# Sums over later key tiles in the third layer: from totals made by VectorE instead of one matmul for each tile

## The reference

```python
def stick_breaking_attention(q, k, v):
    """q, k, v: (B, H, S, Dh). Strictly causal stick-breaking attention, 128-query blocks.
    A[t,s] = sigmoid(z_ts) * prod_{s<j<t} (1 - sigmoid(z_tj)), s < t, evaluated in log space."""
    S = q.shape[2]
    outs = []
    for i in range(S // BLOCK_Q):
        q0, q1 = i * BLOCK_Q, (i + 1) * BLOCK_Q
        qb = q[:, :, q0:q1]
        kb = k[:, :, :q1]
        vb = v[:, :, :q1]
        z = jnp.einsum('bhqd,bhkd->bhqk', qb, kb).astype(jnp.float32) * SB_SCALE
        q_pos = jnp.arange(q0, q1)[:, None]
        k_pos = jnp.arange(q1)[None, :]
        mask = k_pos < q_pos
        log_1m_beta = jnp.where(mask, -jax.nn.softplus(z), 0.0)
        suffix = lax.cumsum(log_1m_beta, axis=3, reverse=True) - log_1m_beta
        w = jnp.where(mask, jnp.exp(jax.nn.log_sigmoid(z) + suffix), 0.0)
        outs.append(jnp.einsum('bhqk,bhkd->bhqd', w.astype(vb.dtype), vb))
    return jnp.concatenate(outs, axis=2)
```

## Time and profile before

| | |
|---|---|
| median of 3 runs | 1201.03 us (1200.93, 1201.03, 2348.67) |
| profiled execution, its own time | 1200.89 us |
| its span, first to last instruction | 1199.1 us |
| PE busy, share of the span | 1188.1 us, 99% |
| DVE busy | 631.9 us, 53% |
| ACT busy | 559.5 us, 47% |
| POOL busy | 415.9 us, 35% |
| granted TensorE clock, mean | 1.000 |

### The profile page before, as it was taken

How to read it: one execution, slowest core, us unless ns; L and a number is a source line. 1 busy time by engine, 2 the same in 40 slices (tenths; PEclk the granted TensorE clock), 3 DMA queues, 4 the chain that set the end, 5 groups by cost and what they waited for, 6 DMA issues and landing times.

```text
span 1199.1 us, 19184 instructions
## 1 busy us (share of the span) xinstructions
PE 1188.1 (99%) x7763; PEld 1019.4 (85%) x7763; DVE 631.9 (53%) x1099; ACT 559.5 (47%) x1071; POOL 415.9 (35%) x295
## 2 busy tenths in 40 slices
PE   8999999999999999999999999999999999999998
PEld 7799879998987778889999888888888888888898
DVE  4587644787577477887370435454442851004434
ACT  5535245535532387886454445454544123344234
POOL 2434331110053255652304323333223553443441
PEclk9999999999999999999999999999999999999999
DMA  8325514557465311002223222212221323323321
GB/s 260 111 71 177 173 36 133 185 170 198 98 130 115 62 36 36 2 2 54 71 71 106 71 71 71 70 40 68 72 71 36 116 95 106 105 88 105 105 71 72
DMA packets 131265, 111.76 MB, mean 93 GB/s; under 512 B 38834, under 2 KB 128048, under 8 KB 131184
## 3 DMA queue, kind: packets, MB, share of 16 engines
q1 hardware_dynamic: 129696, 106.92, 30.7%
q10 hardware_dynamic: 1488, 3.71, 1.4%
HBM read 104.85 MB, written 2.10 MB: 89 GB/s over the span
## 4 chain that ended last, share of the span: by engine, by line
PE 94%; DVE 3%; ACT 2%; DMA 1%; issue 0%; POOL 0%; SPq 0%; ACTq 0%; DVEq 0%
PE banks L1421 43%; PE banks L1410 13%; PE banks L1444 6%; PE banks L1868 4%; PE banks L1886 3%; PE banks L1511 3%; PE banks L2020 3%; PE banks L1849 3%; PE banks L1909 2%; PE banks L2059 2%; PE banks L1982 1%; PE banks L2090 1%; PE banks L1386 1%; PE banks L1581 1%; PE banks L1733 1%; PE banks L1635 1%
## 5 line engine op out<-in xcount | busy, mean ns | idle before, releaser
L672 POOL TENSOR_TENSOR w_lo<-raw,w_hi 128x1024 fp32r<-128x1024 f32 x130 | 325.2, 2522 | 612.3 <-ACT w_hi L775 612.2
L1421 PE MATMUL banks<-act_hi,w_hi 128*128 128x512 f32 x704 | 277.7, 394 | 0.1
L1421 PE MATMUL banks<-act_lo,w_hi 128*128 128x512 f32 x704 | 274.6, 390 | 0.0
L1421 PE MATMUL banks<-act_hi,w_lo 128*128 128x512 f32 x704 | 274.6, 390 | 0.0
L775 ACT ACTIVATE w_hi<-raw 128x1024 fp32r<-128x1024 f32 (+1 forms) x156 | 154.9, 1043 | 124.9 <-PE banks L1421 97.5
L1421 PEld LDWEIGHTS banks<-act_hi,w_hi 128*128 128x128 f32 x704 | 132.4, 188 | 28.2 <-issue 1.4
L1421 PEld LDWEIGHTS banks<-act_lo,w_hi 128*128 128x128 f32 x704 | 132.2, 188 | 28.0
L1421 PEld LDWEIGHTS banks<-act_hi,w_lo 128*128 128x128 f32 x704 | 132.4, 188 | 26.3
L1410 PE MATMUL banks<-w_hi,act_hi 128*128 128x256 f32 x384 | 109.3, 285 | 0.1
L1410 PE MATMUL banks<-w_hi,act_lo 128*128 128x256 f32 x384 | 108.8, 283 | 0.0
L1410 PE MATMUL banks<-w_lo,act_hi 128*128 128x256 f32 x384 | 108.8, 283 | 0.0
(11 more groups left out here) (449 smaller groups left out, 2459.9 us busy)
## 6 DMA issues: line engine op xcount, KB each, us to landing
raw<-w_in SPq DMA_DIRECT2D x32, 1024.0 KB, 5.7
raw<-gla_w_in SPq DMA_DIRECT2D x11, 1024.0 KB, 5.3
raw<-nsa_w_in SPq DMA_DIRECT2D x29, 256.0 KB, 4.5
raw<-nsa_w_in SPq DMA_DIRECT2D x6, 1024.0 KB, 6.6
raw<-gla_w_out SPq DMA_DIRECT2D x4, 1024.0 KB, 6.6
ada_first<-w_ada SPq DMA_DIRECT2D x4, 1024.0 KB, 8.1
raw<-nsa_w_out SPq DMA_DIRECT2D x16, 256.0 KB, 5.1
raw<-w_branch_a SPq DMA_DIRECT2D x4, 1024.0 KB, 5.0
```

Of the source, the lines that this page charges most:

```text
L672: pool.tensor_tensor(w_lo[:, u, k], raw[:, u, k], w_hi[:, u, k].bitcast(F32), ALU.subtract).then_inc(lo_done, 1)
L1421: mm = pe.matmul(b[:], w[:, u, k, m * P:(m + 1) * P], x[:, k, :], start=(k == 0 and n == 0), stop=(k == KT - 1 and n == 2))
```

## The change

`later2` is new: for each head, key tile 2 for query tile 2, and key tile 2 plus key tile 3 for query tile 3. `later1` is key tile 1 plus `later2`, over query tiles 1 to 3. VectorE makes both by two copies and two additions as soon as groups 1 and 2 have their maxima, ahead of their high and low parts and, in pairs 0, 2 and 4, ahead of `query_low`. ScalarE rounds both to `later2_hi` and `later1_hi` between `pair_split(p - 1)` and `take3(c, 1)`, and VectorE makes `later2_lo` and `later1_lo` after group 0's low part. For each head and each of high and low, `head_sums` then needs one matmul with `minus_r` for key tile 1, where two stood (key tiles 2 and 3), and one for key tile 0, where three stood (key tiles 1, 2 and 3). These two sets of four come last in `head_sums`, and each has a wait of its own on `sp_ready`. The new tiles lie in memory of `mix_a` (pairs 0 to 5) and of `qh`, `kh`, `vh` (pairs 6 and 7) that is idle then.

```diff
--- before.py
+++ after.py
@@ -270,6 +270,18 @@
         pool_fix = sb("pool_fix", [P, 4, 16])
         sp_lo = over("sp_lo", [P, 5, S], ln_z, F32R)
         w_z = over("w_z", [P, 5, S], sp_hi)
+
+        def later_parts(name, width, at, last_at, dt=F32R):
+
+            return [over(f"{name}{i}", [P, 2, width], mix_a, dt, at=b)
+                    for i, b in enumerate((mix_a.manual_sbuf_range[0] + 4 * at, last_at))]
+
+        later1_hi = later_parts("later1_hi", 3 * P, 0, qh.manual_sbuf_range[0])
+        later1_lo = later_parts("later1_lo", 3 * P, 6 * P, kh.manual_sbuf_range[0])
+        later1 = later_parts("later1", 3 * P, 6 * P, kh.manual_sbuf_range[0], F32)
+        later2_hi = later_parts("later2_hi", 2 * P, 12 * P, vh.manual_sbuf_range[0])
+        later2_lo = later_parts("later2_lo", 2 * P, 16 * P, vh.manual_sbuf_range[0] + 4 * 4 * P)
+        later2 = later_parts("later2", 2 * P, 16 * P, vh.manual_sbuf_range[0] + 4 * 4 * P, F32)
         pool_u = over("pool_u", [P, KT, S], qh)
         silu_zb = over("silu_zb", [P, KT, S], vh)
         mix_b = over("mix_b", [P, KT, S], ln_z)
@@ -1290,7 +1302,7 @@
                 split_high(c + 1, (c + 1) // 2, (c + 1) % 2)
                 for i, g in enumerate((1, 2, 0)):
 
-                    act.wait_ge(zc_ready, 3 * p + i + 1)
+                    act.wait_ge(zc_ready, 4 * p + i + 1)
                     act.activation(group(ln_z, g), group(ln_z, g), ACT.Exp).then_inc(e_ready, 1)
                 for i, g in enumerate((1, 2, 0)):
                     act.wait_ge(e_ready, 3 * p + i + 1)
@@ -1298,6 +1310,9 @@
                 take3(c, 0)
                 if p:
                     pair_split(p - 1)
+                act.wait_ge(zc_ready, 4 * p + 4)
+                for high, total in ((later2_hi, later2), (later1_hi, later1)):
+                    act.activation(high[p >= 6][:], total[p >= 6][:], ACT.Copy).then_inc(l_ready, 1)
                 take3(c, 1)
                 split_high(c + 2, (c + 2) // 2, (c + 2) % 2)
                 if p % 2 == 0 or p == 7:
@@ -2020,31 +2035,37 @@
                 return pe.matmul(blocks(z_banks, a, st, skip=jt - st), (tri_r if jt == st else minus_r)[:],
                                  blocks((sp_hi, sp_lo)[n], a, jt), start=False, stop=stop, skip_group_check=True)
 
+            def later_sum(a, st, part, p, stop):
+
+                return pe.matmul(blocks(z_banks, a, st, skip=1), minus_r[:], part[p >= 6][:, a], start=False, stop=stop,
+                                 skip_group_check=True)
+
             def head_sums(p):
 
-                pe.wait_ge(sp_ready, 3 * (p + 1))
-                for jt in (3, 2):
-                    for n, part in enumerate((sp_hi, sp_lo)):
-                        pe.matmul(both_heads(z_banks, 2, skip=jt - 2), (tri_r if jt == 2 else minus_r)[:],
-                                  both_heads(part, jt), start=False, stop=(jt == 2 and n == 1), skip_group_check=True)
-                        if jt == 2:
-                            for a in range(2):
-                                source_sum(a, 0, 3, n)
-                for a in range(2):
-                    for n in range(2):
-                        source_sum(a, 1, 2, n)
-                        mm = source_sum(a, 0, 2, n)
+                pe.wait_ge(sp_ready, 5 * p + 3)
+                for part in (sp_hi, sp_lo):
+                    pe.matmul(both_heads(z_banks, 2, skip=1), minus_r[:], both_heads(part, 3),
+                              start=False, stop=False, skip_group_check=True)
+                for n, part in enumerate((sp_hi, sp_lo)):
+                    mm = pe.matmul(both_heads(z_banks, 2), tri_r[:], both_heads(part, 2), start=False, stop=(n == 1),
+                                   skip_group_check=True)
                 mm.then_inc(tri_full, 1)
                 for a in range(2):
                     for n in range(2):
                         source_sum(a, 1, 1, n)
                         source_sum(a, 3, 3, n, stop=(n == 1))
-                        source_sum(a, 0, 1, n)
-                        mm = source_sum(a, 1, 3, n, stop=(n == 1))
-                mm.then_inc(tri_full, 1)
                 for a in range(2):
                     for n in range(2):
-                        mm = source_sum(a, 0, 0, n, stop=(n == 1))
+                        source_sum(a, 0, 0, n)
+                pe.wait_ge(sp_ready, 5 * p + 4)
+                for a in range(2):
+                    for part in (later2_hi, later2_lo):
+                        mm = later_sum(a, 1, part, p, stop=(part is later2_lo))
+                mm.then_inc(tri_full, 1)
+                pe.wait_ge(sp_ready, 5 * p + 5)
+                for a in range(2):
+                    for part in (later1_hi, later1_lo):
+                        mm = later_sum(a, 0, part, p, stop=(part is later1_lo))
                 mm.then_inc(tri_full, 1)
 
             def head_values(p):
@@ -2652,6 +2673,12 @@
                 dve.wait_ge(qk_high, 4 * j + m + 3)
                 dve.tensor_tensor(br_lo[:, 2 * j + m], b, kh[:, j % 2, m].bitcast(F32), ALU.subtract)                    .then_inc(bank_free[2 * ((C_H + 1) % 2) + m], 1)
 
+            def source_split(g):
+
+                link(dve.tensor_copy(group(sp_hi, g), group(ln_z, g)))
+                dve.tensor_tensor(group(sp_lo, g), group(ln_z, g), group(sp_hi, g).bitcast(F32),
+                                  ALU.subtract).then_inc(sp_ready, 1)
+
             for m in range(2):
                 query_low(0, m, bank[2 * (C_H % 2) + m])
             for m in range(2):
@@ -2661,15 +2688,27 @@
 
                     dve.wait_ge(z_full, 3 * p + i + 1)
                     dve.tensor_scalar(group(ln_z, g), group(z_banks, g), CAP, None, ALU.min).then_inc(zc_ready, 1)
-                for i, g in enumerate((1, 2, 0)):
-
-                    if i == 2 and p % 2 == 0 and p < 6:
-                        query_low(p // 2 + 1, 0, bank[0])
-                    dve.wait_ge(l_ready, 3 * p + i + 1)
+                later = (p >= 6)
+                for i, g in enumerate((1, 2)):
+                    dve.wait_ge(l_ready, 5 * p + i + 1)
                     link(dve.tensor_tensor(group(ln_z, g), group(ln_z, g), group(z_banks, g), ALU.max))
-                    link(dve.tensor_copy(group(sp_hi, g), group(ln_z, g)))
-                    dve.tensor_tensor(group(sp_lo, g), group(ln_z, g), group(sp_hi, g).bitcast(F32),
-                                      ALU.subtract).then_inc(sp_ready, 1)
+                source3, source2 = both_heads(ln_z, 3), ln_z[:, 4].rearrange("p (a c) -> p a c", a=2)
+                from2, from1 = later2[later][:], later1[later][:]
+                dve.tensor_copy(from2[:, :, 0:P], source2[:, :, 0:P])
+                link(dve.tensor_tensor(from2[:, :, P:2 * P], source2[:, :, P:2 * P], source3, ALU.add))
+                dve.tensor_copy(from1[:, :, 0:P], ln_z[:, 2:4, 0:P])
+                link(dve.tensor_tensor(from1[:, :, P:3 * P], ln_z[:, 2:4, P:3 * P], from2, ALU.add))
+                dve.sem_inc(zc_ready, 1)
+                for g in (1, 2):
+                    source_split(g)
+                if p % 2 == 0 and p < 6:
+                    query_low(p // 2 + 1, 0, bank[0])
+                dve.wait_ge(l_ready, 5 * p + 3)
+                link(dve.tensor_tensor(group(ln_z, 0), group(ln_z, 0), group(z_banks, 0), ALU.max))
+                source_split(0)
+                for n, (high, low, total) in enumerate(((later2_hi, later2_lo, from2), (later1_hi, later1_lo, from1))):
+                    dve.wait_ge(l_ready, 5 * p + 4 + n)
+                    dve.tensor_tensor(low[later][:], total, high[later][:].bitcast(F32), ALU.subtract).then_inc(sp_ready, 1)
                 if p % 2 == 0 and p < 6:
                     query_low(p // 2 + 1, 1, bank[1])
                 if p:
```

## The result

The changed kernel takes 1208.28 us (median of 5 runs, 1206.61 to 1209.51) against 1200.93 (median of 5, one of which, 2348.67, again stands apart): ratio 1.0061, with a 95% interval of 1.0047 to 1.0075. It is slower, by about 0.6%; the interval leaves out 1, so this is measured, though the prediction counted anything under 2% as no change. The time is inside the forecast range of 1194 to 1211 and 1.6 us above the forecast of 1206.7.

The account below looks back on a forecast made before the run. TensorE was taken as the only limit in the changed stretch; 9.9 us saved against 15.65 lost to waits made it 5.75 us slower, forecast 1206.7 us, range 1194 to 1211.

Parts of the forecast that it names:

- The saving: TensorE's sums: fewer matmuls save 1.24 us for a pair, 9.9 for eight; upper bound 1.45 a pair.
- ScalarE's copies: Two copies ahead of taking product(c)'s second half, about 0.6 and 0.8 us, hidden with 1.1 us of cover.
- The totals: VectorE's two copies and two additions ahead of query_low: 1.6 us, 1.65 with the semaphore count.
- `query_low`'s wait: TensorE waits 1.45 us for query_low before the first half of product(c + 1), in pairs 0, 2 and 4.
- GpSimd's turns: VectorE and GpSimd exclude each other on SBUF, delaying group 0's cast and subtraction; pairs 0, 2, 4 lose 2.85 us each.
- 0.03 us: Pairs 6 and 7: cast ready that long after GpSimd's start, so GpSimd taken as first, 2.8 us lost each.
- rival A: Same as the forecast, but the cast goes ahead of GpSimd in pairs 6 and 7: 1203.5 us; chance 0.20.
- The odd pairs: Cast stays ahead of GpSimd, subtraction and new low parts wait for it: 0.5 us lost each, between 0 and 1.
- B: GpSimd's turns don't hold, group 0's subtraction follows its cast at once: 1195.5 to 1197.7 us; chance 0.14.
- C: VectorE's added work is hidden everywhere: 1191.1 us; chance 0.03.
- D: Odd pairs: cast and subtraction both wait for a whole GpSimd instruction, sums 3 us late: 1214 us; chance 0.10.
- rival E: TensorE's clock falls to 1.2 GHz after pauses, about 5 us more in five pairs: 1232 us; chance 0.04.

Follow-up runs that it names:

- pe_alone: Kernel before with only the shorter sums on TensorE, the last eight matmuls reading their own key tile instead of totals: 1189.49 us, ratio 0.9907.
- both: Changed kernel with query_low ahead of the totals and GpSimd's low part of chunk c + 2 begun after later1_lo: 1189.50 us, ratio 0.9905.
- query_first: Changed kernel with query_low put ahead of the totals, GpSimd as it was: 1210.69 us, ratio 1.0074.
- pause3: Kernel of both, with group 0's maximum made four times instead of once, same result, to make TensorE pause: 1214.72 us, ratio 1.0114.
- dve_alone: Changed kernel with the old 36 matmuls of the sums, the totals and their parts made but read by nothing: 1216.45 us, ratio 1.0134.

## Why the prediction came out as it did

**The saving** was 1.24 us for a pair in the forecast and is 1.39 (pe_alone), 11.2 instead of 9.9 in all; behind a wait 1.27 of it is seen. I had shared out the old sums by width, where 128 columns came to 0.0925 and 384 to 0.1875. What the two cost in turn does not say what each costs alone: in the sums of `both`, 24 matmuls whose widths come to 4.1 by those figures take 3.94. The upper bound, 1.45, held it.

**ScalarE's copies** hide, as forecast: GpSimd's split of pair 2 starts 12.84 us behind the last mask matmul (737.01), where it was 12.85 before.

**The totals** were 1.65 with the semaphore count and took 1.71. `query_low`'s wait was 1.45 and is 1.40 (from 734.96, the start of the matmul ahead, to 736.59, less the usual 0.23).

**GpSimd's turns** went as laid out, instruction by instruction: pairs 0, 2 and 4 lose 2.71 us to the sums instead of 2.85. That this contains `query_low`'s wait and doesn't add to it is what query_first shows. In pairs 6 and 7, where the forecast hung on 0.03 us, GpSimd was first, as taken, by 0.09 us, so rival A is out; with the starts so close, that was partly luck. The loss is 2.69 against 2.8. Pair 6, from the timelines of GpSimd and VectorE:

```profile
868.41 5.16 POOL L684 TENSOR_TENSOR w_lo<-raw,w_hi 128x1024 fp32r<-128x1024 f32 x2 [9.86 <-ACT w_hi L787]
...
868.50 2.86 DVE L2678 CAST sp_hi<-ln_z 128x1024 fp32r<-128x1024 f32 x1
```

The odd pairs lose 0.46 inside the sums instead of 0.5. There the subtraction waits for GpSimd's first instruction and `later2_lo`, the first of the two new low parts, for its second (3.74 us for both, where pair 2 takes 1.54). Pair 1, GpSimd's row and VectorE's:

```profile
705.64 5.76 POOL L684 TENSOR_TENSOR w_lo<-raw,w_hi 128x1024 fp32r<-128x1024 f32 x2 [11.90 <-ACT w_hi L787]
...
705.12 0.69 DVE L2678 CAST sp_hi<-ln_z 128x1024 fp32r<-128x1024 f32 x1
705.85 3.31 DVE L2679 TENSOR_TENSOR sp_lo<-ln_z,sp_hi 128x1024 fp32r<-128x1024 f32 x1
709.08 3.74 DVE L2711 TENSOR_TENSOR later_lo<-later,later_hi 128x512 fp32r<-128x512 f32 x2
```

B falls with these rows, C with `query_low`'s wait, and D because the cast starts 0.52 us ahead of GpSimd's first instruction and keeps its 0.69: only the subtraction waits. (B's upper figure is a slip: by its own terms, 3 x 1.45 and 5 x 0.5, the loss is 6.85 and not 6.6; nothing else hangs on it.) The Trainium skill's rule (SBUF — State Buffer, section Who interferes with whom), that a VectorE instruction with two SBUF inputs or a copy or cast in a two-port mode and a GpSimd instruction that reads SBUF block each other fully, agrees: the subtraction and the cast take 3.30 and 2.26 us with GpSimd at work, 1.23 and 0.69 without.

**The clock** is the term that I had left out of the sum and put at 0.04 as rival E. It is real and smaller than the rival: it fell in pairs 6 and 7 and cost 1.56 us each (5.62 against 4.06), not 5, because it came back within the sums: the stretches behind them are at 1.00 again. That is 3.1 us. The other six pairs came out 0.17 to 0.20 us better than forecast, 1.1 in all, and the last two, the clock apart, 0.14 each. So 1.7 of the 3.1 is left, and that is the miss of 1.6: the forecast came as near as it did in part because errors the other way made up for the clock. The place was wrong too: E had the clock fall behind pauses from 1.4 us on, and behind those of pairs 0, 2 and 4 it never did. The Trainium skill (TensorE: Matmul & The Clock Gate, section Part 1: The HAM clock gate) says that an idle array falls back to 1.2 GHz; the rows at 0.66 behind the long pauses agree, and the row at 1.00 behind pair 7's pause in pause3 shows that a pause of 2.2 us need not bring it about.

## What to carry to other kernels

When work is moved onto VectorE, look at what GpSimd does in the stretch of the timeline where that work, and everything behind it in the queue, will land: here a cast on SBUF that used to start ahead of a GpSimd instruction and now started behind it waited until that one was over, and the subtraction after it waited for the whole of the next. An idle engine's work can then be delayed to make room: one wait on GpSimd turned +0.6% into -0.5%, and an earlier place for one more instruction, `query_low`, made it -0.95%. Where TensorE is the bound, count pauses one by one and not only their sum; a long one can cost more than its length.

## What the runs showed of the hardware that I had not expected

Measured as in the table of pause3, TensorE's pauses of 1.2 to 1.6 us (two in each of three pairs of the changed kernel, one in each of three pairs of pause3) left its granted clock at 1.00; in the profiled executions it fell to the lower level behind most single pauses of 2.2 to 2.9 us: 2 of 2 in the changed kernel, 1 of 2 in dve_alone, 4 of 5 in query_first, 4 of 5 in pause3. Each fall cost 1.4 to 1.6 us. Two pauses alike (pairs 6 and 7 of pause3) went different ways, so what else decides stays open, and so does the share of falls over many executions (query_first's shortest run had about three less than its profiled one). It also makes the time uneven: the changed kernel's five runs, with mean clocks of 0.995 to 0.998, lie over 2.9 us and the longest has the lowest clock, while the version without pauses repeats within 0.12 us. Falls account for most of the 2.9 us and not for all: the profiled 1208.28 already has both long pauses followed by one, and what made 1209.51 longer than that no trace shows.
